# Second mixer: another order under the input tiles, and attention with the scores of two units in PSUM

## What is computed

```python
gate, xr, q, k, v = _split(hx @ w_in, CD_SPLITS)        # and the same for the context
xr = dwconv_centred(xr, conv_w, conv_b)
h, _, _ = rglru_bidir(xr, wa, ba, wx, bx, lam_p, hf_c, hb_c)   # gated scan, both ways
q, k = rms_norm per head, then apply_rope
s = einsum('bqhtd,bkhtd->bhtqk', qb, k) * d ** -0.5     # t: two maps a head
p = softmax(s);  w = p[:, :, 0] - lam * p[:, :, 1]
o = einsum('bhqk,bkhe->bqhe', w, v);  o = rms_norm(o, subln_g) * (1 - lam_init)
y = concatenate([gelu(gate) * h, o]) @ w_out
```

## Time and profile before

| what | us |
|---|---|
| median of 3 runs | 2978.83 (2975.6 to 2981.44) |
| the profiled execution | 2978.31 |
| its span, first to last instruction | 2976.5 |
| PE busy in it | 2806.0 (94%) |
| input tiles with the work under them, 2270 to 2476: PE busy | 176.04 of 206 |
| attention in its steady part, 2502 to 2545: PE busy | 35.00 of 43 |

### The profile page before, as it was taken

How to read it: one execution, slowest core, us unless ns; L and a number is a source line. 1 busy time by engine, 2 the same in 40 slices (tenths; PEclk the granted TensorE clock), 3 DMA queues, 4 the chain that set the end, 5 groups by cost and what they waited for, 6 DMA issues and landing times.

```text
span 2976.5 us, 41142 instructions
## 1 busy us (share of the span) xinstructions
PE 2806.0 (94%) x15844; PEld 2634.7 (89%) x15844; DVE 1542.5 (52%) x2043; ACT 1107.6 (37%) x1527; POOL 570.1 (19%) x294
## 2 busy tenths in 40 slices
PE   5999999999977789999999999999999887899999
PEld 5899999998965678999999999999998666788887
DVE  6964366454556856662465542222256556653333
ACT  3432144236455334441343332123324765442221
POOL 2441044200012721440343100000021320100000
PEclk8999999999999889999999999999999999999999
DMA  7343144111220012442343121211212110123232
GB/s 299 128 156 122 59 150 165 65 50 50 70 43 1 1 33 96 162 166 67 122 160 108 48 64 63 71 56 63 72 58 69 43 57 15 40 92 102 92 97 100
DMA packets 68392, 258.77 MB, mean 87 GB/s; under 512 B 7504, under 2 KB 9424, under 8 KB 67792
## 3 DMA queue, kind: packets, MB, share of 16 engines
q1 hardware_dynamic: 50736, 192.58, 19.6%
q10 hardware_dynamic: 17568, 65.02, 6.3%
HBM read 255.47 MB, written 2.10 MB: 87 GB/s over the span
## 4 chain that ended last, share of the span: by engine, by line
PE 83%; DVE 8%; issue 3%; ACT 3%; POOL 1%; DMA 0%; DVEq 0%; ACTq 0%; POOLq 0%
PE G L446 20%; PE G L450 20%; PE G L448 20%; PE G L453 5%; PE G L455 5%; PE G L457 5%; DVE B L1491 1%; PE G L870 1%; DVE wl L1486 1%; DVE tmp L1675 1%; PE NP L753 1%; DVE sL L1895 1%; DVE xl L1667 1%; PE NP L662 1%; DVE sL L1886 0%
## 5 line engine op out<-in xcount | busy, mean ns | idle before, releaser
L987 ACT ACTIVATE wh<-raw 128x1024 fp32r<-128x1024 f32 (+1 forms) x300 | 338.6, 1129 | 1473.2 <-PE G L450 1174.4
L446 PE MATMUL G<-xh,wh 128*128 128x384 f32 x2624 | 676.4, 338 | 33.3 <-DVE wl L1486 21.0
L448 PE MATMUL G<-xl,wh 128*128 128x384 f32 x2624 | 670.1, 336 | 0.0
L450 PE MATMUL G<-xh,wl 128*128 128x384 f32 x2624 | 669.5, 336 | 0.0
L1486 DVE TENSOR_TENSOR wl<-raw,wh 128x1024 fp32r<-128x1024 f32 (+1 forms) x300 | 424.6, 1415 | 386.8 <-ACT wh L987 386.1
L446 PEld LDWEIGHTS G<-xh,wh 128*128 128x128 f32 x2624 | 475.6, 189 | 42.7 <-DVE wl L1486 18.4
L448 PEld LDWEIGHTS G<-xl,wh 128*128 128x128 f32 x2624 | 477.2, 189 | 0.0
L450 PEld LDWEIGHTS G<-xh,wl 128*128 128x128 f32 x2624 | 477.1, 189 | 0.0
L2218 POOL TENSOR_TENSOR mraw<-mraw,scb 128x1024 f32<-128x1024 f32 x120 | 315.2, 2627 | 646.5 <-DVE B L1491 646.5
L446 PE MATMUL G<-hh,wh 128*128 128x384 f32 x1056 | 267.9, 334 | 0.0
L450 PE MATMUL G<-hh,wl 128*128 128x384 f32 x1056 | 267.9, 334 | 0.0
(11 more groups left out here) (352 smaller groups left out, 3298.3 us busy)
## 6 DMA issues: line engine op xcount, KB each, us to landing
raw<-in_w SPq DMA_DIRECT2D x176, 512.0 KB, 3.5
mraw<-in_wmn ACTq DMA_DIRECT2D x120, 512.0 KB, 4.4
raw<-in_w SPq DMA_DIRECT2D x64, 704.0 KB, 4.0
raw<-in_abin SPq DMA_DIRECT2D x24, 512.0 KB, 3.5
raw<-in_cdin SPq DMA_DIRECT2D x20, 512.0 KB, 3.5
mini<-in_wmn SPq DMA_DIRECT2D x9, 512.0 KB, 14.8
gmini<-in_wmn SPq DMA_DIRECT2D x2, 2048.0 KB, 22.0
raw<-in_about SPq DMA_DIRECT2D x8, 512.0 KB, 3.6
```

What stands on the lines that cost most here:

```text
L446: pe.matmul(bank(h), W, tokens(rh, h), start=(k == 0), stop=False)
L448: pe.matmul(bank(h), W, tokens(rl, h), start=False, stop=False)
L450: mm = pe.matmul(bank(h), L, tokens(rh, h), start=False, stop=(k == nk - 1))
L987: act.activation(wh[slot][:, 0:nk * P], raw[slot][:, 0:nk * P], ACT.Copy).then_inc(hi_done, 1)
```

## The change

Two parts. Under the input tiles: the gate's gelu is taken out of the evacuation (a plain copy) and done once for all four tiles later (`gelu`); products with the gate and their split are done once too; exp and tanh of a scan block are spread over two tiles; sigmoids wait for the last product that reads their target (`lru_b`) and not for the block's whole scan (`lru_h`); the convolution of block 3 and the fourth scan stand elsewhere; head sums, swaps and v transposes have other places in the tables.

In attention `SC[0]` and `SC[1]` take three banks each, so that two units' scores lie in PSUM. T and V now share the last two banks (`B67`), V in one place for all units. S(a) is cut in two parts around V(a-3). M is one instruction for both maps. Step a is now, on PE, S(a) first part, V(a-3), S(a) second part, T(a-2); on DVE, M(a), W(a-1), O(a-3); on ACT, C(a-2), E(a), squares(a-4). T(a) waits for `on_done` a, that is O(a-1). The end is changed too: 12 heads are normed ahead of the last units, and the transposes of the result stand between the last units and the first four chunks of the output matmul.

```diff
-        ATT = (TB, XL + 4 * TX)
+        ATT = (TB, XL)
...
-        G = [ctx.enter_context(nc.psum_tensor(f"G{s}", [P, 1024], F32)) for s in range(2)]
-        NP = ctx.enter_context(nc.psum_tensor("NP", [P, 1024], F32))
-        B67 = ctx.enter_context(nc.psum_tensor("B67", [P, 1024], F32))
+        banks = ctx.enter_context(nc.psum_tensor("banks", [P, 4096], F32))
+        G = [banks[:, 1024 * s:1024 * s + 1024] for s in range(2)]
+        NP, B67 = banks[:, 2048:3072], banks[:, 3072:4096]
+        SC = [banks[:, 1536 * q:1536 * q + 1536] for q in range(2)]
...
-        SUM_AT = {(10, 3): 0, (12, 2): 1, (13, 4): 2, (14, 4): 3, (15, 2): 4, (16, 2): 5, (17, 2): 6, (18, 2): 7}
+        SUM_AT = {(10, 3): 0, (12, 0): 1, (14, 4): 2, (15, 4): 3, (16, 2): 4, (17, 2): 5, (18, 2): 6, (19, 1): 7}
...
-                        if c in GATES_IN and k in (2, 6):
-                            gates(GATES_IN[c], k // 4)
+                        if c in GATES_IN and k in (2, 5 if c < 8 else 4):
+                            gates(GATES_IN[c], int(k > 2))
...
-                def scores(a):
+                def scores(a, part):
                     qt, h = a // 4, a % 4
-                    for s in range(2):
-                        if a == 0:
-                            pe.wait_ge(psum_free[s], CDO // 2)
-                        else:
-                            pe.wait_ge(p2_ready, 2 * a + s - 1)
-                    if a < 4:
-                        pe.wait_ge(rope_done, 5 + a)
-                    for b_ in range(0, T, 256):
-                        for s in range(2):
-                            hp = slice(64 * s, 64 * s + 64)
-                            mm = pe.matmul(G[s][:, b_:b_ + 256], q2[hp, h, P * qt:P * qt + P], k2[hp, h, b_:b_ + 256],
-                                           start=True, stop=True)
-                            if b_ == 512:
-                                mm.then_inc(s2_done, 1)
+                    if part == 0:
+                        if a < 2:
+                            for s in range(2):
+                                pe.wait_ge(psum_free[s], CDO // 2)
+                        if a == 1:
+                            pe.wait_ge(v2_ready, 3)
+                        if a >= 2:
+                            pe.wait_ge(p2_ready, 2 * a - 2)
+                        if a < 4:
+                            pe.wait_ge(rope_done, 5 + a)
+                    for s, b_ in ((0, 512), (1, 256), (0, 0), (1, 512), (0, 256), (1, 0))[3 * part:3 * part + 3]:
+                        hp = slice(64 * s, 64 * s + 64)
+                        if (s, b_) == (1, 0):
+                            pe.wait_ge(s2_bank, a + 1)
+                        mm = pe.matmul(SC[a % 2][:, T * s + b_:T * s + b_ + 256], q2[hp, h, P * qt:P * qt + P],
+                                       k2[hp, h, b_:b_ + 256], start=True, stop=True)
+                        if (s, b_) == (0, 512):
+                            mm.then_inc(s2_bank, 1)
+                    if part:
+                        mm.then_inc(s2_done, 1)
 
                 def turn(a):
                     pe.wait_ge(w_done, a + 1)
                     if a:
-                        pe.wait_ge(wt_ready, a)
+                        pe.wait_ge(on_done, a)
                     else:
-                        pe.wait_ge(v2_ready, 3)
+                        pe.wait_ge(v2_ready, 4)
                     for k in range(NT):
-                        mm = pe.transpose(NP[:, P * k:P * k + P], wb[a % 2][:, P * k:P * k + P], cst("ident"))
+                        mm = pe.transpose(B67[:, P * k:P * k + P], wb[a % 2][:, P * k:P * k + P], cst("ident"))
                     mm.then_inc(tr2_done, 1)
 
                 def values(a):
                     pe.wait_ge(wt_ready, a + 1)
-                    if a >= 2:
-                        pe.wait_ge(on_done, a - 1)
-                    else:
-                        pe.wait_ge(v2_ready, 4)
                     h = a % 4
                     for k in range(NT):
-                        mm = pe.matmul((B6, B7)[a % 2][:, 0:P], wtb[a % 2][:, P * k:P * k + P],
+                        mm = pe.matmul(B67[:, T:T + P], wtb[a % 2][:, P * k:P * k + P],
                                        vtok[:, k, P * h:P * h + P], start=(k == 0), stop=(k == NT - 1))
                     mm.then_inc(pv2_done, 1)
 
                 for a in range(NA2 + 3):
                     if a < NA2:
-                        scores(a)
+                        scores(a, 0)
+                    if 3 <= a:
+                        values(a - 3)
+                    if a < NA2:
+                        scores(a, 1)
                     if a == 0:
+                        swap(7)
+                        turn_v(1)
                         turn_v(2)
                         turn_v(3)
                     if 2 <= a <= NA2 + 1:
                         turn(a - 2)
-                    if 3 <= a:
-                        values(a - 3)
...
-                def gelu(i):
+                def evac_gate(i):
 
                     act.wait_ge(mm_done, CD + 4 + i + 1)
-                    act.activation(gate[:, i, :], G[i % 2][:, 0:NLAT], ACT.Gelu_apprx_tanh).then_inc(psum_free[i % 2], 1)
+                    act.activation(gate[:, i, :], G[i % 2][:, 0:NLAT], ACT.Copy).then_inc(psum_free[i % 2], 1)
+                def gelu():
+                    act.wait_ge(psum_free[0], (CD + 6) // 2 + 1)
+                    act.wait_ge(psum_free[1], (CD + 6) // 2 + 1)
+                    act.activation(gate[:], gate[:], ACT.Gelu_apprx_tanh).then_inc(gate_set, 1)
 
...
+                def sigmoids(p_, d):
+                    if p_:
+                        act.wait_ge(lru_b, 2 * p_ - 1 + d)
+                    for g, (dst, bias) in enumerate(((lR, "lba"), (lI, "lbx"))):
+                        act.wait_ge(gate_mm, 4 * p_ + 2 * d + g + 1)
+                        if p_ and g:
+                            act.wait_ge(scan_l, 2 * p_ - 1 + d)
+                        act.activation(dst[d][:], (NP, B67)[g][:, 0:T], ACT.Sigmoid,
+                                       bias=pr(bias)[:, 4 * d + p_:4 * d + p_ + 1]).then_inc(gate_sig, 1)
...
-                    if a < NA2:
-                        for s in range(2):
-                            act.wait_ge(max2_ready, 2 * a + s + 1)
-                            if a >= 2:
-                                act.wait_ge(w_done, a - 1)
-                            act.activation(pr2[a % 2][s][:], G[s][:, 0:T], ACT.Exp, bias=st2[:, a % 4, s:s + 1],
-                                           accum_out=st2[:, a % 4, 2 + s:3 + s]).then_inc(p2_ready, 1)
                     if 2 <= a <= NA2 + 1:
                         act.wait_ge(tr2_done, a - 1)
                         if a >= 4:
                             act.wait_ge(pv2_done, a - 3)
-                        act.activation(wtb[a % 2][:], NP[:, 0:T], ACT.Copy).then_inc(wt_ready, 1)
+                        act.activation(wtb[a % 2][:], B67[:, 0:T], ACT.Copy).then_inc(wt_ready, 1)
+                    if a < NA2:
+                        act.wait_ge(max2_ready, a + 1)
+                        if a >= 2:
+                            act.wait_ge(w_done, a - 1)
+                        for s in range(2):
+                            act.activation(pr2[a % 2][s][:], SC[a % 2][:, T * s:T * s + T], ACT.Exp, bias=st2[:, a % 4, s:s + 1],
+                                           accum_out=st2[:, a % 4, 2 + s:3 + s]).then_inc(p2_ready, 1)
                     if a >= 4:
...
+                        head_squares(a - 4)
...
+                    if c == 3:
+                        conv(2)
+                        conv(3)
                     if c == 4:
...
-                def att(a):
-                    if a >= 4:
-                        b = a - 4
-                        dve.wait_ge(pv2_done, b + 1)
-                        dve.tensor_scalar(onq[b // 4][:, P * (b % 4):P * (b % 4) + P], (B6, B7)[b % 2][:, 0:P],
-                                          st2[:, b % 4, 4:5], None, ALU.mult).then_inc(on_done, 1)
-                    if a < NA2:
-                        for s in range(2):
-                            dve.wait_ge(s2_done, 2 * a + s + 1)
-                            dve.tensor_reduce(st2[:, a % 4, s:s + 1], G[s][:, 0:T], AX.X, ALU.max, negate=True
-                                              ).then_inc(max2_ready, 1)
...
+                def out(b):
+                    dve.wait_ge(pv2_done, b + 1)
+                    dve.tensor_scalar(onq[b // 4][:, P * (b % 4):P * (b % 4) + P], B67[:, T:T + P],
+                                      st2[:, b % 4, 4:5], None, ALU.mult).then_inc(on_done, 1)
+                def biggest(a):
+                    dve.wait_ge(s2_done, a + 1)
+                    dve.tensor_reduce(st2[:, a % 4, 0:2], SC[a % 2].rearrange("p (s t) -> p s t", s=2), AX.X, ALU.max,
+                                      negate=True).then_inc(max2_ready, 1)
...
+                for a in range(NA2 + 2):
```

(55 more changed lines are left out.)

254 lines of the change are left out of this document (128 added, 126 removed).

## The result

The changed kernel takes 3032.68 us (median of 4, 3032.33 to 3032.96), the kernel before 2978.35 beside it (2975.6 to 2981.44): 1.018 times as long, with a 95% interval of 1.016 to 1.020, 54 us slower. The profiled execution took 3032.93 us.

What follows compares the result with a forecast made beforehand. PE was taken as the bound, 83% of the last-ending chain. 2978.3 - 22 (input tiles) + 35.4 (attention ring) + 9 (clock) + 2 (end) = 3002.7, so 3003 us, 0.8% slower; 8 in 10 range 2987 to 3023.

Steps and rivals of the forecast that it cites:

- Faster: Rival in attention: second place for scores works, PE never waits for DVE, step 4.1 us, total 2949; chance 0.06.
- The input tiles, 22 gained: Under the input tiles: 16.6 us of PE waits and 5.6 of lower clock go; bounds 11 to 33.6.
- the low part of weights at L453: Under the input tiles: PE's waits for it were 6.1 us, one of 4.8, which was taken as gone.
- the sigmoid: Under the input tiles: PE's wait of 6.1 us for a sigmoid behind a table load, taken as gone.
- the head sums: Under the input tiles: PE's 11.6 us of waits for the low part of a head's squares; 7 kept, 4.6 gained.
- four groups of 25.9 us: PE's waits under the input tiles: squares' low part 11.6 us, sigmoid 6.1, weights' low part 6.1, gate tile's bank 2.1.
- The ring, 7.70 us: Attention: DVE's and PE's steps run in turn, 7.70 us a step against 4.58, 12 steps, 37.4 us lost; step bounds 7.3 to 7.9.
- The three steps ahead of it, 13 us: Attention's three steps before the ring closes: 15.0 us before, 13 after, 2 gained.
- The clock in attention, 9 us: Waits of 3.5 us a step lower PE's clock in 5 or 6 of 14 steps: 9 us lost, nothing to 28.
- My row of 2.97 us: Earlier kernel's trace: third scores waited 2.97 us and took 1.67; the fourth took 2.93 instead of 1.57.
- The end, 2 lost: Last M to first output matmul: 18.2 us before, 19.7 after plus about 0.5 of wait; 2 lost, bounds -2 to 5.
- mostly at the lower level: Rival in attention: clock term 28 us in place of 9, total 3022, or 3033 with half the input gain; chance 0.15.

Runs made afterwards that it cites:

- 20 transposes: The changed kernel with 20 useless transposes of the identity added on PE ahead of T(1) to T(13): 2993.45 us, 1.006 of before.
- O first: The changed kernel with O(a-3) moved ahead of M(a) and W(a-1) on DVE: 2947.94 us, 0.990 of before.
- both fillings: The changed kernel with useless transposes added on PE ahead of T(1) to T(13): 20 of them 2993.45 us, 8 of them 3010.09 us.
- the other four: Changed kernel with DVE order M, O, W: 2991.02 us; with old attention: 2952.53; O moved ahead of M, S cut four and two: 2942.73; another end on top: 2937.17.

## Why the prediction was right and wrong

**The direction and the place were right.** T waits for O in each step, 13 waits of 3.58 us (I said 3.5, some 14), and the experiment that the prediction named as the deciding point, O ahead of M on DVE, gave 2948 us, where the rival *Faster* had 2949. So that rival named the right condition for a kernel one instruction away from this one. That its time fits to 1 us is in part luck: its step was 4.1 and came out as 4.45, its start was to gain 22 and gained 26. DVE waited 6.8 us for scores and not 4, since PE's part of the ring is longer at the lower clock; at the full clock, with 20 transposes, the same wait is 4.68.

**The input tiles, 22 gained: right, and a little low.** In the whole kernel the gain up to the first M was 26.1, 4 more than the term and inside its bounds. Alone the input tiles gave 22.4 by the medians; that this is the very number is luck, since it has the 2.5 us put off in it. PE's idle time under them is 11.2 us of 179 (I said 8 to 13 of 185). By terms: the wait for the bank is gone; that for the low part of weights at L453 fell from 6.1 to 0.5, where I took 4.8 off; the sigmoid kept 3.2 of the 6.1 that I took as gone whole; the head sums fell to 4.7 where I kept 7. The errors nearly cancel: four groups of 25.9 us became 8.4, which is 17.5 gained where I had 16.6.

**The ring, 7.70 us: 0.38 short.** At the full clock it is 8.08. By its parts: DVE with the way to PE 3.66 (I had 3.60), T up to V 1.83 (1.82), V 1.53 (1.42), the second part of S 1.06 (0.86). I had the two rounds of three matmuls right, 2 x 0.43, and left out the 0.20 that each part takes on top; why V takes 0.1 longer no run says. The 1.83 is also T and the first part of S, 0.77 + 1.06, so this piece fits by C as well as by PE's own work. 12 x 0.38 = 4.6 us. The three steps ahead of it, 13 us, were right.

**The clock in attention, 9 us: this is the step that failed.** I wrote "so I take 5 or 6 of 14", each at the 1.70 us of the shortest stretch. All 12 steps lost, 2.4 to 3.9 us and 2.99 on average: 35.9 us, 26.9 more than the term and 8 more than its upper bound of 28. Two things were wrong in it. One step does 4.4 us of PE work, and in all 12 steps T (1.51) and the first part of S (2.07), and more than half or all of V (2.35 to 2.93), ran at 0.50, which is more than 1.70 us' worth. And I reasoned that 4 us of work without pause brings the clock back and counted that as more than half of the steps unharmed. It does come back in nine of the 12 (the second part of S takes 1.13 in six and 1.23 to 1.26 in three, but 2.07 in the other three), only late in the step, and the next wait of 3.58 us follows at once. The very row that I took the price from, 3.40 us of PE work without a pause at 0.50, shows that work alone doesn't bring it back at once. My row of 2.97 us, with the slow scores behind it, should have weighed more than the waits of 0.87 that leave the clock alone. The Trainium skill's rule that I set beside this term ("TensorE: Matmul & The Clock Gate", HAM oscillation: a loop that waits in every round begins each one cold) agrees with the trace after: T, the first work behind each of the waits of 3.58 us, takes 1.51 us in place of 0.87, and the granted clock is 0.65 through the 12 steps.

**The end, 2 lost: 2.0 up to the first output matmul,** and 1.0 at the fifth chunk, where I had put 0.5. Behind it lie 1.8 us in the last 408 that no part of the change touches; the profiled executions of the experiments show 406.7 to 406.8 there (O first, both fillings) or 408.2 to 408.4 (the other four), whatever their attention is like; the cause stays open.

Sum of the misses against 3002.7: 4.6 + 26.9 for the ring and its clock, 4.1 less at the start, 1.0 + 1.8 at the end: 30.2 us, and 3032.9 is what the profiled execution took.

The rival *mostly at the lower level* had 3022 and 3033; its mechanism is the one that came, with 0.15. Its 3033 is luck, since it counts on half the gain at the input and the whole came; its price of 28 us was 8 short too. The other page of the Trainium skill that I named, "Perfetto Trace Analysis", section on matmuls, wants independent groups to rotate through PSUM banks. Here T and V share one place in every kernel with O first, and PE was busy for all of 53.46 and of 48.44 us. So the order on DVE decided; T and V didn't need to rotate. The rival's other way, T in another bank with DVE's order left as it is, was not run.

## What to carry to other kernels

Follow a new wait through the queue of both engines before you count what a second buffer frees: if the releasing instruction stands behind one that needs what is queued behind the waiting one, the two engines run in turn, and one moved instruction can be worth more than the whole change (85 us here, where the change lost 54). If a loop on TensorE waits as long as here in each round (3.58 us, with 4.4 us of work), price most of its work in the round at the lower clock, and not one short stretch in some rounds: all of it would have been 53 us more in 12 steps, and 35.9 came. When scores of 64 rows are cut in parts, cut them in pairs, and as seldom as can be: each part took 0.20 us of its own.

## What the hardware did that I had not expected

- More work was faster: 20 useless transposes a step took 39 us off, 35.9 of them in the 12 steps, where the granted clock went from 0.65 to 1.00.
- The price of the clock is not smooth in the wait. With 3.58 us each step lost, and executions agreed within 0.6 us; with 1.25 us left none did; with 2.20 and 2.56 us some steps did and some not, and eight executions of one kernel lay 31 us apart (2981.6 to 3012.45).
- Three of these 64-row matmuls and four of them take the same 1.06 us.
